# Hybrid mLSTM / attention / PEER step on one core: a later place for the fourth tile's projection, ring slots for tile 0's weights, and an early half of the first scores

## The reference, cut to what matters

```
h = rmsnorm(x);  proj = h @ w_in                        # 1024 -> 2824 columns
hm = mlstm(proj part);  hs = windowed attention(proj part)
x = x + concat(hm, hs) @ w_out                          # 1024 x 1024
h2 = rmsnorm(x);  q = h2 @ w_q                          # 1024 -> 2048: 8 heads, 2 halves
s1, s2 = q halves . sub_keys                            # 128 scores each, per head and half
t1,i1 = top16(s1); t2,i2 = top16(s2); top = top16(all 256 sums); idx = the 16 expert numbers
a = gelu(u[idx] . h2)                                   # 16 gathered rows of 1024 floats per row and head
x = x + sum over heads and k of softmax(top) * a * v[idx]
y = rmsnorm(x)
```

## Time and profile before

| what | value |
|---|---|
| median of 3 runs | 3343.56 us (3331.28 to 3344.0) |
| the profiled execution | 3339.74 us, its span 3337.9 us |
| PE busy | 2578.6 us (77%) |
| DVE busy | 2077.5 us (62%) |
| POOL busy | 1995.5 us (60%) |
| ACT busy | 578.7 us (17%) |
| DMA | 1193.69 MB, mean 358 GB/s |

### The profile page before, as it was taken

The page is one execution under the profiler, slowest core; times in us unless marked ns, Lnnn a source line. Parts: engine busy times, 40 slices in busy tenths (PEclk is TensorE's granted clock), DMA queues, the critical chain, the costliest instruction groups (busy, mean ns, idle before and its releaser), DMA issues.

```text
span 3337.9 us, 34528 instructions
## 1 busy us (share of the span) xinstructions
PE 2578.6 (77%) x11351; PEld 1054.6 (32%) x11351; DVE 2077.5 (62%) x5202; ACT 578.7 (17%) x1055; POOL 1995.5 (60%) x2128
## 2 busy tenths in 40 slices
PE   8993797678667999956876797779777886789655
PEld 4562233234223533312432242223322341225111
DVE  1116766776676556645667776776677666765653
ACT  2201212211121211112122112121112111211111
POOL 0003666766776556645567677676766676755775
PEclk9996888889888999987888898888887897776878
DMA  5045999999999999999899999999999999998998
GB/s 189 29 166 176 388 342 394 401 384 391 407 396 375 392 361 409 385 385 357 307 354 409 388 402 408 395 397 370 408 398 378 373 409 394 408 355 294 394 409 330
DMA packets 341418, 1193.69 MB, mean 358 GB/s; under 512 B 37680, under 2 KB 46776, under 8 KB 339192
## 3 DMA queue, kind: packets, MB, share of 16 engines
q0 software_dynamic: 304128, 1107.43, 85.1%
q1 hardware_dynamic: 37112, 84.05, 6.7%
HBM read 1175.84 MB, written 15.60 MB: 357 GB/s over the span
## 4 chain that ended last, share of the span: by engine, by line
PE 39%; DMA 21%; DVE 13%; POOL 13%; issue 7%; DVEq 4%; ACT 2%; SPq 1%; ACTq 1%; POOLq 0%
DMA ring<-in_peer_u_dram,idx 12%; PE acc L1402 11%; POOL ring L488 7%; DVE ring L1074 6%; POOL ring L480 6%; DMA ring<-in_peer_v_dram,idx 6%; PE mx L1317 6%; PE acc L1141 5%; PE mx L1307 4%; PE acc L1369 3%; PE mx L1156 3%; PE h2p L1347 2%; DVEq L982 2%; PE acc L1358 2%; DMA proj_scratch<-weights 1%
## 5 line engine op out<-in xcount | busy, mean ns | idle before, releaser
L1402 PE MATMUL acc<-ring,wk 128*32 128x512 f32 x4224 | 1246.5, 722 | 486.9 <-DMA ring<-in_peer_v_dram,idx 446.8
L1074 DVE SCALAR_TENSOR_TENSOR ring<-ring,h2p 128x1024 f32<-128x1024 f32 x1056 | 1280.1, 1215 | 534.5 <-DMA ring<-in_peer_u_dram,idx 441.9
L480 POOL DMA_INDIRECT ring<-in_peer_u_dram,idx x1056 | 996.5, 944 | 784.3 <-DVEq L1030 274.8
L488 POOL DMA_INDIRECT ring<-in_peer_v_dram,idx x1056 | 996.8, 944 | 538.9 <-issue 273.0
L1402 PEld LDWEIGHTS acc<-ring,wk 128*32 128x32 f32 x4224 | 252.1, 123 | 1315.2 <-issue 1240.8
L1317 PEld LDWEIGHTS mx<-reg,weights 128*128 128x128 f32 x2304 | 279.9, 202 | 74.3 <-issue 73.1
L1317 PE MATMUL mx<-reg,weights 128*128 128x128 f32 (+1 forms) x2304 | 293.7, 288 | 3.8 <-DVEq L961 1.6
L1369 PE MATMUL acc<-xt,ident 32*32 32x512 f32 x132 | 102.6, 920 | 89.9 <-DVEq L1043 89.9
L1141 PE MATMUL acc<-weights,ring 128*128 128x512 f32 (+1 forms) x384 | 159.4, 574 | 0.0
L1307 PE MATMUL mx<-weights,reg 128*128 128x512 f32 (+1 forms) x288 | 142.5, 650 | 0.0
L669 ACT ACTIVATE gl<-dots 128x16 f32<-128x16 f32 x66 | 14.2, 216 | 728.6 <-DVEq L1077 728.5
(11 more groups left out here) (263 smaller groups left out, 2181.6 us busy)
## 6 DMA issues: line engine op xcount, KB each, us to landing
weights<-in_w_in_dram SPq DMA_DIRECT2D x10, 2048.0 KB, 19.0
ring<-in_peer_u_dram,idx POOLq DMA_INDIRECT x1056
ring<-in_peer_v_dram,idx POOLq DMA_INDIRECT x1056, 8.2
weights<-in_peer_w_q_dram SPq DMA_DIRECT2D x8, 2048.0 KB, 11.5
weights<-in_w_out_dram SPq DMA_DIRECT2D x2, 4096.0 KB, 19.2
proj_scratch<-weights SPq DMA_DIRECT2D x20, 256.0 KB, 6.1
pj<-proj_scratch SPq DMA_DIRECT2D x7, 644.0 KB, 14.3
xt<-in_x_prompt_dram SPq DMA_DIRECT2D x8, 512.0 KB, 6.7
```

Source lines behind the costliest of these rows:

```text
L480: pool.indirect_dma_start(ring[:, n % NU, :], None, u_d, bass.IndirectOffsetOnAxis(ap=idx[:, g % 4, k:k + 1], axis=0)).then_inc(u_in[n % N ...
L488: pool.indirect_dma_start(ring[:, NU + n % NV, :], None, v_d, bass.IndirectOffsetOnAxis(ap=idx[:, g % 4, k:k + 1], axis=0)).then_inc(v_in[ ...
L1074: V.scalar_tensor_tensor(ring[:, n % NU, :], ring[:, n % NU, :], 1.0, h2p[:, :], ALU.mult, ALU.mult, accum_out=dots[:, (g + 1) % 2, k:k + ...
L1402: last = T.matmul(acc[j:j + SUB, cols], wk[:, g % 2, i, :], ring[:, NU + (TOPK * g + i) % NV, cols], start=not own and g % 2 == 0 and i == ...
```

## The change

1. Only tiles 0 to 2 are projected ahead. The stages of tile 0 lie between the chunks of tiles 1 and 2, by the new table EARLY_AT (ten bounds in place of a division).
2. Chunk 0 of tile 3 is projected behind tile 0's `out_proj`. Chunks 1 to 5 are projected in loop -1, at the steps of LAST_PE, and copied at the steps of LAST_ACT and LAST_DVE to new places (`po_last`: `part` and the v slots 5 and 6 of the ring).
3. Tile 0 reads w_out from the ring (two halves, slots 4 to 11, loaded near 35 us), and w_q from the ring (eight pieces of 256 columns in four buffers). The loads of w_out and w_q to `weights` remain, for tile 1 on: they come with the chunks of tile 3, now in loop -1.
4. After 8 of the 16 queries PE takes the scores of group 0 alone (`score_first`), ACT copies them (`keep_first`), and DVE starts topk(0). Queries 8 to 15 and the other scores come after it; `spread_rows(0)` stands after query 11.
5. topk(2) moves from loop -1 to loop 0, which does two stages in a step; loop -1 does one.
6. New waits: POOL's u gather 4 on query 11; v gather 5 on the stores of chunks 2 and 3 of tile 3, v gather 6 on those of 4 and 5; PE's first sums in `acc` on the last chunk copies; ACT's first use of `part` on the stores of chunks 0 and 1; `load_p(1)` stands ahead of the stores of tile 3.

```diff
+EARLY_AT = (10, 14, 20, 24, 32, 36, 41, 46, 50, 53)
+LAST_PE = {0: 1, 2: 2, 5: 3, 8: 4, 11: 5}
+LAST_ACT = {7: 2, 12: 4}
+LAST_DVE = {4: 1, 11: 3, 15: 5}
...
-            out.setdefault(NC_ + r * 16 // EARLY_END, []).append((s, i, 0))
+            out.setdefault(NC_ + sum(r >= a for a in EARLY_AT), []).append((s, i, 0))
...
+        wout_first = [ring[:, 4 + 4 * b:8 + 4 * b, :]... for b in range(2)]
+        wq_first = [ring[:, 4 + 2 * b:6 + 2 * b, :]... for b in range(4)]
+        po_last = [(part, ring[:, NU + 5, :], ring[:, NU + 6, :])[c // 2][:, c % 2 * 512:c % 2 * 512 + PC[c][1]] for c in range(NC_)]
...
+            def load_wout_first(b):
+                sp.dma_start(wout_first[b], w_out[0, :, b * 512:b * 512 + 512]...).then_inc(wout_first_in[b], 16)
+            def load_wq_first(j):
+                sp.dma_start(wq_first[j % 4], w_q[0, :, j * 256:j * 256 + 256]...).then_inc(wq_first_in[j % 4], 16)
...
+            sp.wait_ge(first_used, 1)
+            load_wq_first(0)
+            load_wq_first(1)
+            sp.wait_ge(mixed_ready, 1)
+            load_wq_first(2)
+            load_wq_first(3)
+            store_proj(FIRST - 1, 0)
+            sp.wait_ge(first_used, 2)
+            load_wq_first(4)
...
             for c in range(NC_):
+                sp.wait_ge(proj_out[c], 16 * 2)
+            load_p(1)
+            for c in range(1, NC_):
                 sp.wait_ge(chunk_ready, NC_ * (FIRST - 1) + c + 1)
                 if c == 1:
                     load_wout()
-                elif c > 1:
+                else:
                     load_wq(2 * (c - 2))
                 store_proj(FIRST - 1, c)
...
+                elif n == NU - 1:
+                    pool.wait_ge(query_ready, 3)
...
+                elif n >= NV - 2:
+                    for c in (2, 3) if n == NV - 2 else (4, 5):
+                        pool.wait_ge(proj_out[c], 16 * (FIRST - 1))
...
+            def keep_first():
+                act.wait_ge(first_scored, 1)
+                act.wait_ge(proj_out[0], 16 * (FIRST - 2))
+                S.copy(sc[:, 0:2, :]..., mx[:, 0, 0:2 * NK])
...
                     if g < 0:
+                        if k <= 10:
+                            topk(1, k)
+                        if k in LAST_DVE:
+                            chunk_copy(FIRST - 1, LAST_DVE[k])
+                    elif g == 0:
                         for stage in (2 * k, 2 * k + 1):
                             if stage < 22:
-                                topk(1 + stage // 11, stage % 11)
+                                topk(2 + stage // 11, stage % 11)
...
+            def score_first():
+                pe.wait_ge(qT_ready, 2)
+                for c in range(8):
+                    ...
+                last.then_inc(first_scored, 1)
...
-            for m in range(FIRST):
+            for m in range(FIRST - 1):
                 proj_tile(m)
             for s, i, r in PE_AT:
                 if r >= EARLY_END:
                     mix(s, i, 0)
-            spread_rows(0)
+                    if s == "out_proj" and i == 7:
+                        project(FIRST - 1, 0)
+                    if s == "query" and i == 7:
+                        score_first()
+                    if s == "query" and i == 11:
+                        spread_rows(0)
```

More of the change, by code:

```diff
@@ L229, in program @@
         x1 = [ring[:, b, :] for b in range(2)]
-        hT1 = [ring[:, 2 + b, :].rearrange("p (k t) -> p k t", k=DC) for b in range(2)]
         tail = DC * COLS
+        hT1 = [a.rearrange("p (k t) -> p k t", k=DC) for a in (ring[:, 2, :], weights[:, tail:tail + D])]
+        wout_first = [ring[:, 4 + 4 * b:8 + 4 * b, :].rearrange("p a d -> p (a d)").rearrange("p (k c) -> p k c", k=DC) for b in range(2)]
+        wq_first = [ring[:, 4 + 2 * b:6 + 2 * b, :].rearrange("p a d -> p (a d)").rearrange("p (k c) -> p k c", k=DC) for b in range(4)]
         x1_again = reg[:, 1024:2048]
@@ L1323, in mix @@
                     if i * SUB < n:
-                        for c in range(QC):
+                        for c in range(8 if m == 0 and i == 0 else 0, QC):
                             q, col = c // 2 % 4 * SUB, (c // 8 * 2 + c % 2) * NK
@@ L1328, in mix @@
                             last.then_inc(keys_scored, 1)
+            def score_first():
+                pe.wait_ge(qT_ready, 2)
+                for c in range(8):
+                    q = c // 2 * SUB
+                    last = T.matmul(mx[q:q + SUB, 0, c % 2 * NK:(c % 2 + 1) * NK], qT[:, c, 0:SUB], kT[:, c % 2, :], start=True, stop=True)
+                last.then_inc(first_scored, 1)
             def final_weights():
```

77 lines of the change are left out of this document (62 added, 15 removed).

## The result

The changed kernel takes **3300.06 us** (median of four runs, 3287.95 to 3304.49) against 3343.78 us (four runs, 3331.28 to 3344.27) before: a ratio of **0.9872, 95% interval 0.9848 to 0.9896**, or 43 us less. The profiled execution is the fastest of its four: 3287.95 us, span 3286.2 us, 51.7 us under the span before. The interval lies clear of 1, so the change is faster, by 1.3%. The forecast was 3302 us in a range of 3280 to 3328, faster.

What follows compares the result with a forecast made beforehand. Gathers filling the DMA engines bound the kernel, their start set by a chain of waits. Sums of -36 us (-65.6 + 33.7 - 4.3) and -42 with 3 for DVE gave -38: 3339.7 - 38 = 3302 us, range 3280 to 3328.

Steps and rivals of the forecast that it cites:

- What bounds it: Whole kernel: gathers fill the DMA engines from 350 us on; first gather, bytes and idle DMA after it set the end.
- Part 1: PE ahead of tile 0's end: six fewer chunks and one wait gone, -45 us, range -38 to -46.
- Part 2: w_out and w_q for tile 0 through the ring, in idle DMA time: 0 us, at worst 5 us.
- Part 3: Chunk 0 in PE's 5.78 us gap at the norm: transposes pushed 1.1 us and giving it back, queries at 184.4 us.
- Part 4 and 5: Scores after half the queries, then DVE's waits: first gather 65.6 us earlier at 212.2, other dots 58 us earlier from 225.4.
- Part 6: Weight loads and stores now beside gathers: 13.8 MB cost +33.7 us, less idle gives -4.3; sum -36 us.
- Part 7: POOL's v gather 6 waits for chunk 5's store: out at 295 us, -42 us, with 3 us charged for DVE.
- Part 7's second reckoning: Store ahead of v gather 6, w_out and w_q loads landing one behind the other in median times: 65 us, landing at 296.
- No repayment in bytes (3282): Rival, chance 0.13: DMA engines find room later for the loads, only the dots' -58 us counts, 3282 us.
- DVE and a slow PE (3320): Rival, chance 0.20: slow-clocked chunks 2 to 5 and bare topk stages in loop 0 leave -20 us, 3320 us.
- The last store held (3405): Rival, chance 0.06: loads land singly in longest times, store at 400 us, v gather 6 65 us later, 3405 us.

Runs made afterwards that it cites:

- e3: Kernel before with 11.5 MB of w_out and w_q loads to weights cut out, ahead of its first gather: 3636.24 us, ratio 1.0000 to the kernel before.
- e2: Changed kernel with 11.5 of the 12.6 MB of w_out and w_q loads beside the gathers cut out: 3565.84 us, ratio 0.9831 to the kernel before.
- e11: Changed kernel with all four w_q loads issued behind the last store of tile 3, so v gathers wait for nothing: 3292.19 us, ratio 0.9859.
- e1: Changed kernel run again without edit, on a slower chip: 3592.34 us, ratio 0.9907 to the kernel before on that chip.
- e4: Changed kernel with each store of tile 3's chunks 2 to 5 issued ahead of its step's w_q load: 3573.65 us, ratio 0.9852.
- e6: Changed kernel with topk(2) put back into loop -1, two stages a step: 3579.39 us, ratio 0.9836.
- e8: The kernel of e4 run again in the second batch: 3579.54 us, ratio 0.9840 to the kernel before.
- e9: Kernel before with only the early scores of group 0 after 8 queries added: 3331.14 us, ratio 0.9967.
- e5: Changed kernel without the early scores of group 0, so topk(0) waits for the whole copy: 3599.39 us, ratio 0.9888.
- e12: The kernel of e11 with topk(2) put back into loop -1, as in e6: 3302.27 us, ratio 0.9882.
- e7: Changed kernel with topk(1)'s stages two steps later in loop -1: 3600.44 us, ratio 0.9877.
- e10: Changed kernel run again without edit, in the third batch: 3297.47 us, ratio 0.9861 to the kernel before.

## Why the prediction was right, step by step

**What bounds it** held: the shift arises in the first 300 us, and from 350 us on share and rate are those of the earlier trace rows.

**Part 1** was too small. The last mixing work of tile 0 started at 156.52 us (159.8 expected) and out_proj at 158.49 (161.8): -48.7 us where I took -45.4, outside its own range. The wait that goes (6.03 us) and the new one (2.41 us at 104.33 against "about 2") were as read. What I left out is what the idle time did behind itself. The granted clock of before, in the 10 us behind that gap and behind the gap at the norm:

```profile
165.00:175.00 10.00, 10.00 (x29) 6.30 (x30) 0.21 (x2) 1.07 (x2) 0.00 (x0) 0.70 0.01 2
...
230.00:240.00 10.00, 10.00 (x65) 10.00 (x66) 0.00 (x0) 0.00 (x0) 0.00 (x0) 0.71 0.00 0
```

0.30 of 10 us is 3 us for the first. The passes themselves say the same. Behind the gap of before come 16 transposes and two chunks, and the same work is found after at the full clock. The transposes took 3.47 us before (164.87 to 168.34) and 1.75 after (132.06 to 133.81), and two chunks, before and then after:

```profile
168.34 15.22 PE L1141 MATMUL acc<-weights,ring 128*128 128x512 f32 x32
```

```profile
118.22 14.00 PE L1213 MATMUL acc<-weights,ring 128*128 128x512 f32 x32
```

That is 1.7 + 1.2 = 2.9 us of the missing 3.3; after, the clock is 1.00 from 100 us to out_proj.

**Part 2** held: the ring pieces of w_q landed in 5.7 us in the median and 8.2 at most, and the queries never waited.

**Part 3** held at the gap (chunk 0 at 172.33, transposes 1.04 us as expected) and missed the second line above: the queries took 14.53 us for eight, 1.82 each, where I carried over the 1.98 of the earlier trace rows, whose first 10 us ran at 0.71. The two together, 3.3 us at out_proj and 1.4 in the first eight queries, are nearly all of the 4.8 us by which the first gather came early. The Trainium skill ("TensorE: Matmul & The Clock Gate", on the clock gate) has the clock fall after idle time and rise under load. These rows agree: 0.70 behind 6.03 us of idle time, 0.71 behind the 5.78 us at the norm, and 1.00 where the change has closed both. I had cited it only for a rival, against the change, and not for the gaps that the change closes.

**Part 4 and 5**: first gather at 207.35 us (212.2 expected) by those two gains, topk(1)'s first stage at 219.31 (225.4). The order of events was the forecast's.

**Part 6's mechanism** was right in kind: e3 shows the bytes free ahead of the gathers, e2 shows them paid for beside them, though with 12.6 to 18.5 us of 28 by group 4, not in full. Its sum was off: -36 us against 48 to 51. Two terms were off, the start by -4.8 us and the idle time, and the price of the bytes, which I charged in full, may be a third. I had 10 us of idle DMA behind the first gather; the stretches give 4.65 x 0.42 + 20 x 0.05 + 55 x 0.03 = 4.6 us, because six gathers of 0.52 MB and tile 1's load kept the engines at 0.95 from 212 to 232 us, where I had counted 5.5 + 1.5 us idle. Measured the same way, before has 15.4 us (the second stretch adds 0.6). Put in, -70.4 + 33.7 - 10.8 + 3.5 for tile 1's 1.4 MB, which I had left out, is -44 us, and the observed rate of 400 to 421 GB/s beside loads, a little better than the average of the gathers, may cover some of the rest; no run separates it.

**Part 7** named the right wait at the right place. Its v gather 6 was due at 295 us and came at 285.86, 48.7 us earlier than before, and that is the shift which stayed (-49.7 at group 4, -51.4 at the end). The 9 us by which it was early come from the start (6.1 us earlier at topk(1)) and from the 3 us that I had added for POOL to fill the queue again. The term most off behind that is the 3 us charged for DVE in loop 0: e11, which has no wait for the stores, is 5 to 8 us earlier at group 4. The loss is small since the DMA engines are full meanwhile.

Part 7's second reckoning, the 296 us by the medians of the earlier trace rows laid end to end, came near by luck. The medians mix two cases. Of the eight w_q loads of before, four ran ahead of the gathers and landed in 7.7 to 11.9 us, and four ran beside gathers near 1450 us and landed in 8.4 to 36.0. The 4 MB load of w_out took 13.2 us in the first case and 25.1 in the second. In loop -1 of the changed kernel the four w_q loads took 24.2 to 31.6 us each and w_out 21.8, but they were in flight together. The rows near 1450 us also were a case of two full queues, which the prediction said no row showed.

**The rivals.** No repayment in bytes (3282) falls by e2's group times. DVE and a slow PE (3320) falls by the timeline: chunks 1 to 4 took 14.00 and 13.90 us a pair, at a granted clock of 1.00, and DVE didn't wait for chunk 5. The last store held (3405) falls: the w_q loads of loop -1, issued from 231.51 to 251.86 us, landed in 31.6 us at most, so they overlapped, and v gather 6, which waits for the last store, left 28.8 us after that store's issue at 257.07.

**The total.** I forecast -38 us from the profiled execution. The medians differ by 43.7 us and the two profiled executions by 51.8, of which the one after is the fastest of its four, and those spread over 16 us. So the change was underrated by 6 us by the medians, and 3302 lies as near to 3300 as it does partly because before's profiled execution, from which I counted, is 4 us under its median.

**Open**: how much of their DMA time the 12.6 MB cost in the end, since e2's lead is 26.5 us over e1 and 7.8 over e4 by the medians; whether the 0.005 to 0.007 in the ratio of e4, e6 and e8 over e1 are more than scatter, as their intervals touch or overlap e1's; what DVE's stops in e1 are; whether e11 would gain on the slower chips, which wasn't tried.

## What to carry to other kernels

Where a queue of transfers bounds the rest, count a change at the start in bytes: what is done ahead counts fully, and bytes moved from idle DMA time to beside the gathers are paid for, here with half to two thirds of their time by group 4 (e2, e3). An edit's worth depends on the wait behind it: the same part moved v gather 6 by 11 us alone and by 1.4 in company (e9, e5), and the same move of topk(2) cost nothing ahead of a wait and 6 to 7 us without it (e6, e12), so measure it in the place where it stays. Before a run is taken as a base, look in its profile for stops that belong to no edit: e1's made the edits of e4, e6 and e7 look 4 to 6 us better than they are, and the part that e5 takes out as much cheaper. When a gap on PE is closed, count the slow clock behind the gap too.

## What the runs showed of the hardware

The same kernel took 3342 to 3344 us on some chips and 3632 to 3643 on others, about 9% more, with gathers at 382 and 350 GB/s. Where loads run beside gathers both kinds reach as much (417 to 421 GB/s in three stretches of 10 us in the first result, 419 over 40 us in e1), and from 10 to 30 us, where only loads run, both read 383 to 387: it is the gathers alone that are slower there. A 0.26 MB store behind 2 MB loads in SP's queue landed after up to 29.3 us, where 2.0 is its median, and a 2 MB load of w_q beside gathers in loop -1 took 26.9 us in the median, against 9.6 for the four that ran before the first gather in the kernel before. That fits what the prediction cited of the Trainium skill ("DMA: Bandwidth & Descriptors", on queues, rings and completion order): both queues go on, each slower, and a store waits its turn within its own. Line L359 after:

```profile
DMA to landing us min/median/max: 1.7/2.0/29.3
```

e10's six runs lie at 3288 to 3290 us and at 3305 to 3308, three and three, with nothing between: more than e11 could be expected to differ by. The same wait of PE, 2.41 us near 104 us (2.40 in e7), was followed by a granted clock of 1.00 over 104 to 108 us in the first result, e1, e10 and e11 and of 0.63 to 0.73 in e6, e7 and e12. No run shows why.
